# TensorE's expert loop gets one turn ahead of the first expert, and the rank products and the first gather stand inside it

## The chip, the cores and the metric

One core of one Trainium2 chip runs the kernel, one launch. The metric is the device time of that core in microseconds, the median of the runs; smaller is better.

## What is computed

Two transformer blocks over 256 tokens of width 1024, in f32. The change touches the last stage, a mixture of 32 experts, of which every token uses four:

```
logits = t @ w_router + b_router
top_val, top_idx = lax.top_k(logits, TOP_K)          # 4 of 32
gate_w = jax.nn.softmax(top_val, axis=-1)
...
xb = t_pad[tok_idx]                                   # the tokens of one expert
hb = xb @ w_exp_in[e] + b_exp_in[e]                   # 1024 x 2048
g, u = jnp.minimum(hb[:, :F], 7.0), jnp.clip(hb[:, F:], -7.0, 7.0)
a = g * jax.nn.sigmoid(1.702 * g) * (u + 1.0)
return a @ w_exp_out[e] + b_exp_out[e]                # 1024 x 1024
...
y = jnp.einsum('nk,nkd->nd', gate_w, y_slot)
```

## The kernel before

The weights of an expert are 12 MB: 8 MB of `w_exp_in` (in `big_mem`, four pieces of two rows k, semaphores `win_in`) and 4 MB of `w_exp_out` (four pieces, `wout_in`). There is one place for them on the chip. The queue of SyncE (SP) writes a piece of the next expert (L430, L433) as soon as TensorE (PE) has counted up `gu_part` or `y_part` for the piece that it replaces. The first expert's pieces are loaded before the loop (L413, L416).

Before the loop PE sums the logits; VectorE (DVE) makes from them the choice `sel` (L2022, `sel_ready`) and the gates. PE then multiplies `sel` with a triangle and with ones (L908 to L912: the rank of each token in its expert, `rank_ps`), transposes the gates (L917), and DVE makes from the ranks the selection `picks` of the first expert (L2040). With it PE gathers that expert's tokens (L1025, L1026; the matmuls stand in L936). Then PE reads from `further` how many tokens the first expert has, and enters `pe.Fori(0, E)` at L1071.

A turn of the loop is one expert. Its body holds the same pass three times, written out for up to 32, 64 and 96 tokens (`GROUPS[0]`, `[1]`, `[2]`), and conditional branches jump over those that don't apply: L1083 over the first, L1086 over the second, L1088 over the third; L1096 jumps over `bias_out`, and L1071 goes back to the loop's start. A pass is: the first product (`gu`, L953, waits for `win_in`), the gather of the next expert's tokens (L936), transposes (L974, L982), the second product (`second`, L994, waits for `wout_in`) and the sum into the output banks (`combine`, L1008, L1017). The first expert in the loop takes the pass for 64 tokens, the second that for 32. DVE, ScalarE (ACT) and SP have loops of their own, which the change leaves as they are.

PE's program is read in blocks of 16 KB by a DMA queue of its own (q8, kind "instruction").

Of the kernel before, what the change touches and what calls it, by code (L numbers as in the profile page):

```python
# [16 lines left out]
P = 128  # L17
D = 1024
SEQ = 256
T = SEQ // P  # L20
KD = D // P
# [4 lines left out]
E = 32  # L26
# [4 lines left out]
TRIO = 3  # L31
SLOTS = TRIO * XS
PASSES = -(-SEQ // SLOTS)
TURNS = E + -(-SEQ * 4 // SLOTS) + 1
EARLY = 5
GROUPS = (((0, XS),), ((0, 2 * XS),), ((0, 2 * XS), (2 * XS, XS)))
# [85 lines left out]
def program(nc, ins, out):  # L122
# [3 lines left out]
    with ExitStack() as ctx:  # L126
        s = {n: ctx.enter_context(nc.semaphore(n)) for n in EVENTS}
# [114 lines left out]
        sel = sb("sel", T, E)  # L242
        gate = sb("gate", T, E + 1)
# [6 lines left out]
        further = sb("further", 2, E + 1, dt=I32)  # L250
# [3 lines left out]
        order = sb("order", E + 1, dt=I32)  # L254
# [3 lines left out]
        ident = stay[:, IDENT:IDENT + P]  # L258
        aeye = stay[:, AEYE:AEYE + P]
        tri = stay[:, TRI:TRI + P]  # L260
        ones = stay[:, ONES:ONES + P]

        ps = ctx.enter_context(nc.psum_tensor("ps", [P, 8, 512], F32))
# [213 lines left out]
        def _(pe):  # L477
            mm = nc.tensor.matmul
# [130 lines left out]
            for g in range(2):  # L609
                for k in range(KD):  # L610
                    for z in range(2):
                        mm(ps[HEAD * z:HEAD * (z + 1), 2, SEQ * g:SEQ * (g + 1)], cols8[1][:, k, HEAD * g:HEAD * (g + 1)], hT[:, k, :],
                           start=(k == 0), stop=(k == KD - 1))
            for t in range(T):
                for k in range(KD):
                    last = mm(ps[:, 3, P * t:P * (t + 1)], hT[:, k, P * t:P * (t + 1)], cols8[1][:, k, P:2 * P],
                              start=(k == 0), stop=(k == KD - 1))
# [27 lines left out]
            for r in range(2):  # L645
                b = 4 + 2 * r
                pe.wait_ge(s["pv_out"], 3 + r)
                for m in range(2):
                    hd = 2 * r + m
                    mm(ps[:, b + m, 0:SEQ], m1["krT"][:, hd, 0:P], m1["qrT"][:, hd, :], start=True, stop=True)  # L650
                    last = mm(ps[:, b + m, SEQ:KEYS], m1["krT"][:, hd, P:SEQ], m1["qrT"][:, hd, P:SEQ], start=True, stop=True)
                last.then_inc(s["inner_ps"], 1)
            for r in range(2):
                b = 4 + 2 * r
                pe.wait_ge(s["decay_ready"], r + 1)
                for m in range(2):
# [5 lines left out]
                    last = mm(ps[:, b, SEQ + P * m:SEQ + P * (m + 1)], w[:, SEQ:KEYS], v[1], start=False, stop=True)  # L662
# [14 lines left out]
            for hd in range(RET_HEADS):  # L677
                for t in range(T):
                    last = nc.tensor.transpose(ps[:, 5 + 2 * (hd // 2), 256 * (hd % 2) + P * t:256 * (hd % 2) + P * (t + 1)],
                                               m1["ret"][:, t, P * hd:P * (hd + 1)], ident)  # L680
# [19 lines left out]
            with pe.Fori(0, NF // 2) as j:  # L700
                for u in range(2):
                    pe.wait_ge(s[f"conv{u}"], j + 1)
                    for g in range(2):
                        b = 2 * u + g
                        pe.wait_ge(s[f"lo{b}"], j + 1)
                        for k in range(KD):
                            if u == 0 and g == 0 and k % 4 == 0:
                                pe.wait_ge(s["hT_lo"], KD + 2 * k)
                            last = three(ps[:, 4 + u, SEQ * g:SEQ * (g + 1)], quarter(w_hi, b)[:, k, :], quarter(w_lo, b)[:, k, :],
                                         hT_hi[:, k, :], hT_lo[:, k, :], k == 0, k == KD - 1)  # L710
# [22 lines left out]
            for t in range(T):  # L733
                for n in range(2):
                    for k in range(NF - 4, NF):
                        if t == 0 and n == 0:
                            pe.wait_ge(s[f"lo{k % 4}"], NF // 2 + k // 4 + 1)
                        last = down(k, t, [n])
# [8 lines left out]
            for i in range(4):  # L747
                last = mm(ps[:, i, :], stay[:, FLIP:FLIP + P], toep_flipped[:, 2 * i:2 * i + 2, :], start=True, stop=True)
# [76 lines left out]
            for hd in range(4):  # L825
                for t in range(T):
                    last = nc.tensor.transpose(ps[:, hd // 2, 256 * (hd % 2) + P * t:256 * (hd % 2) + P * (t + 1)],
                                               m2["oD"][:, t, P * hd:P * (hd + 1)], ident)
# [3 lines left out]
            for i in range(4):  # L832
                for side, (x_hi, x_lo, x_ready, w_ready) in enumerate(((oa_hi, oa_lo, "oa_lo", "c_lo_a"), (ob_hi, ob_lo, "ob_lo", "c_lo_b"))):
                    p = 2 * i + side
# [38 lines left out]
            for t in range(T):  # L873
                for q in range(4, 8):
                    pe.wait_ge(s["q_lo"], q - 1)
                    last = closing(q, t)
# [27 lines left out]
            for n in range(2):  # L904
                residual(1, n)

            pe.wait_ge(s["sel_ready"], 1)
            mm(ps[:, 5, 0:E], tri, sel[:, 0, :], start=True, stop=True)  # L908
            mm(ps[:, 5, E:2 * E], ones, sel[:, 0, :], start=True, stop=False)
            mm(ps[:, 5, E:2 * E], tri, sel[:, 1, :], start=False, stop=True)  # L910
            mm(ps[:, 5, 2 * E:3 * E], ones, sel[:, 0, :], start=True, stop=False)
            mm(ps[:, 5, 2 * E:3 * E], ones, sel[:, 1, :], start=False, stop=True).then_inc(s["rank_ps"], 1)  # L912


            pe.wait_ge(s["gates_done"], 1)
            for t in range(T):
                last = nc.tensor.transpose(ps[0:E, 4, P * t:P * (t + 1)], gate[:, t, 0:E], ident)  # L917
            last.then_inc(s["gateT_ps"], 1)

            def bias_out():  # L920

                pe.wait_ge(s["gateT_ready"], 1)
# [8 lines left out]
            def gather(lo, hi, bank=7):  # L931

                for k in range(lo, hi):
                    c = SLOTS * (k % EARLY)
                    for t in range(T):
                        last = mm(ps[:, bank, c:c + SLOTS], h1[:, t, SEQ * (k // 2) + k % 2:SEQ * (k // 2 + 1):2], moe["picks"][:, t, :], start=(t == 0), stop=(t == T - 1))  # L936
                if hi in (EARLY, KD):
                    last.then_inc(s["gather_ps"], 1)
# [82 lines left out]
                        pe.wait_ge(s["combined"], 2 * nth + 2)  # L1021

            pe.sem_inc(s["combined"], 1)
            pe.wait_ge(s["picks_ready"], 1)
            gather(0, EARLY)  # L1025
            gather(EARLY, KD, 6)  # L1026
            pe.wait_ge(s["gateT_ready"], 1)
            pe.wait_ge(s["counts_ready"], 1)
            pe.wait_ge(s["bias_zeroed"], 2)
            pe.wait_ge(s["bias_split"], 2)  # L1030
            base_reg, turn_reg = pe.alloc_register("pe_base"), pe.alloc_register("pe_turn")
            pe.reg_mov(base_reg, 0)
            pe.reg_mov(turn_reg, 0)
# [1 line left out]
            def one_pass(blocks, landed_all, load_next):  # L1035

                base = pe.snap(base_reg, min_val=0, max_val=2 * TURNS)
                turn = pe.snap(turn_reg, min_val=0, max_val=2 * TURNS)
                pe.wait_ge(s["xT_ready"], 2 * turn + 1)
                pe.wait_ge(s["own_ready"], turn + 1)  # L1040
                gu(blocks, landed_all, 2 * turn + 2)
                pe.wait_ge(s["picks_ready"], turn + 2)
                gather(0, EARLY)
                load_next()
                for b, (at, m) in enumerate(blocks):
                    pe.wait_ge(s["source_ready"], base + b + 1)
                    pe.wait_ge(s["u_ready"], base + b + 1)
                    way_back(b, at)
                for b, (at, m) in enumerate(blocks):
                    pe.wait_ge(s["back_ready"], base + b + 1)  # L1050
                    pe.wait_ge(s["a_ready"], base + b + 1)
                    turn_a(at, m)
                pe.wait_ge(s["xT_ready"], 2 * turn + 3)
                gather(EARLY, EARLY + 1)
                pe.wait_ge(s["aT_ready"], base + len(blocks))
                second(blocks, landed_all)
                gather(EARLY + 1, EARLY + 2)
                for b, (at, m) in enumerate(blocks):
                    pe.wait_ge(s["y_ready"], base + b + 1)
                    combine(b, at, m, base + b)  # L1060
                gather(EARLY + 2, KD)
                pe.reg_add(base_reg, base_reg, len(blocks))
                pe.reg_add(turn_reg, turn_reg, 1)

            extra_reg, more_reg, next_extra, next_more = (pe.alloc_register("pe_" + z) for z in ("extra", "more", "next_extra", "next_more"))
            pe.reg_mov(extra_reg, pe.value_load(further[0:1, 0, 0:1], min_val=0, max_val=TRIO - 1))
            pe.reg_mov(more_reg, pe.value_load(further[0:1, 1, 0:1], min_val=0, max_val=PASSES - 1))
            nth_reg = pe.alloc_register("pe_nth")
            for r in (next_extra, next_more, nth_reg):
                pe.reg_mov(r, 0)  # L1070
            with pe.Fori(0, E) as e:  # L1071
                landed_all = 16 * e + 16
                extra = pe.snap(extra_reg, min_val=0, max_val=TRIO - 1)
                more = pe.snap(more_reg, min_val=0, max_val=PASSES - 1)

                def load_next():

                    pe.wait_ge(s["order_ready"], 1)
                    following = pe.value_load(order[0:1, bass.ds(e + 1, 1)], min_val=0, max_val=E)
                    pe.reg_mov(next_extra, pe.value_load(further[0:1, 0, bass.ds(following, 1)], min_val=0, max_val=TRIO - 1))  # L1080
                    pe.reg_mov(next_more, pe.value_load(further[0:1, 1, bass.ds(following, 1)], min_val=0, max_val=PASSES - 1))

                with pe.If(extra < 1):  # L1083
                    one_pass(GROUPS[0], landed_all, load_next)
                with pe.If(extra > 0):
                    with pe.If(extra < 2):  # L1086
                        one_pass(GROUPS[1], landed_all, load_next)
                    with pe.If(extra > 1):  # L1088
                        with pe.Fori(0, PASSES) as p:
                            with pe.If(more >= p):  # L1090
                                one_pass(GROUPS[2], landed_all, load_next)
                            pe.nop()
                        pe.nop()
                    pe.nop()
                pe.nop()
                with pe.If_eq(nth_reg, E // 2):  # L1096
                    bias_out()
                pe.reg_add(nth_reg, nth_reg, 1)
                pe.reg_mov(extra_reg, next_extra)
                pe.reg_mov(more_reg, next_more)  # L1100
# [1113 lines left out]
```

## Time and profile before

| | |
|---|---|
| median of 3 runs | 1506.52 us (1506.22 to 1511.2) |
| the profiled execution | 1507.34 us |
| its span | 1505.5 us |
| mean granted TensorE clock | 0.976 |
| PE busy | 1339.8 us (89%) |
| DVE, ACT, POOL busy | 448.4, 359.8, 139.0 us |
| read from HBM | 492.76 MB, 328 GB/s over the span |
| q8, instruction | 26 packets, 0.43 MB |

The span runs from the first to the last instruction of the profiled execution, whose own time is 1.8 us longer. The experts' weights are 384 MB of the 493 MB read. A stall of the engine's instruction stream shows in the profile as idle time "issue" before the engine's next instruction, and as the duration of the branch itself on the sequencer (PEldq).

### The profile page before, as it was taken

The numbers are of one execution on the slowest core, as the hardware profiler recorded it, in microseconds if no ns is written. First come the engines' busy times: TensorE is split into PE (matmuls) and PEld (weight loads), VectorE is DVE, ScalarE is ACT, GpSimd is POOL, SyncE is SP. The second block draws the span as 40 slices with busy tenths as digits, with TensorE's granted clock in tenths as the row PEclk, the third lists the DMA queues.
The fourth block names the chain that finished last, engine by engine and source line by source line (L and its number), as shares of the span: only waits on it lengthen the run. The fifth ranks groups of instructions, "written<-read, shape, count | busy, mean of one in ns | idle before, by whom it ended". The sixth has DMA issues, their size and how long they took to land.

```text
span 1505.5 us, 25303 instructions
## 1 busy us (share of the span) xinstructions
PE 1339.8 (89%) x9344; PEld 801.1 (53%) x9345; DVE 448.4 (30%) x906; ACT 359.8 (24%) x690; POOL 139.0 (9%) x65
## 2 busy tenths in 40 slices
PE   7999999998999898988998888998889988889865
PEld 6454999887989863434343333343334333433432
DVE  1326677745543771111111111111011111111112
ACT  1234666545566520101000100010001001000101
POOL 0000122005765400000000000000000000000000
PEclk9999999999999999999999999999999999999997
DMA  9442466855344478999999999999999999999996
GB/s 342 152 129 56 118 190 181 320 195 187 135 147 168 168 285 364 429 425 427 424 411 426 429 426 426 424 412 425 427 424 428 411 425 426 428 428 424 407 427 258
DMA packets 113493, 494.35 MB, mean 328 GB/s; under 512 B 7617, under 2 KB 55089, under 8 KB 80465
## 3 DMA queue, kind: packets, MB, share of 16 engines
q1 hardware_dynamic: 111971, 491.50, 81.5%
q10 hardware_dynamic: 1486, 2.34, 0.4%
q8 instruction: 26, 0.43, 0.1%
q14 instruction: 10, 0.08, 0.0%
HBM read 492.76 MB, written 1.06 MB: 328 GB/s over the span
## 4 chain that ended last, share of the span: by engine, by line
PE 59%; DMA 33%; DVE 3%; ACT 2%; issue 2%; SPq 0%; DVEq 0%; ACTq 0%
DMA big_mem<-in_w_exp_in 29%; PE ps L953 16%; PE ps L994 6%; PE ps L696 5%; PE ps L698 5%; PE ps L697 5%; PE ps L524 4%; PE ps L936 4%; DMA big_mem<-in_w_exp_out 3%; PE ps L668 2%; PE ps L720 1%; PE ps L722 1%; PE ps L721 1%; PE ps L1017 1%; PE ps L513 1%
## 5 line engine op out<-in xcount | busy, mean ns | idle before, releaser
L953 PE MATMUL ps<-big_mem,ring_mem 128*32 128x512 f32 (+1 forms) x2304 | 382.4, 640 | 67.7 <-DMA big_mem<-in_w_exp_in 67.7
L953 PEld LDWEIGHTS ps<-big_mem,ring_mem 128*32 128x32 f32 (+1 forms) x2304 | 112.6, 125 | 313.2 <-issue 200.8
L994 PE MATMUL ps<-big_mem,x 128*32 128x256 f32 (+1 forms) x1888 | 181.9, 430 | 8.3 <-DMA big_mem<-in_w_exp_out 4.5
L696 PE MATMUL ps<-hT_hi,w_hi 128*128 128x256 f32 x600 | 171.2, 285 | 1.3 <-DVE hT_lo L1619 1.3
L936 PEld LDWEIGHTS ps<-ring_mem,h 128*128 128x128 f32 x1056 | 137.3, 200 | 62.5 <-issue 61.3
L698 PE MATMUL ps<-hT_hi,w_lo 128*128 128x256 f32 x600 | 169.8, 283 | 0.0
L697 PE MATMUL ps<-hT_lo,w_hi 128*128 128x256 f32 x600 | 169.8, 283 | 0.0
L936 PE MATMUL ps<-ring_mem,h 128*128 128x96 f32 x1056 | 154.7, 291 | 0.9 <-DVE ring_mem L2040 0.9
L2081 DVE TENSOR_SCALAR ring_mem<-ps 128x256 f32<-128x256 f32 (+1 forms) x36 | 18.7, 520 | 429.9 <-PE ps L953 429.9
L1524 ACT ACTIVATE ring_mem<-ring_mem 128x256 f32<-128x256 f32 (+1 forms) x36 | 17.7, 493 | 492.0 <-DVE ring_mem L2081 492.0
L994 PEld LDWEIGHTS ps<-big_mem,x 128*32 128x32 f32 (+1 forms) x1888 | 70.6, 115 | 105.8 <-issue 64.7
L696 PEld LDWEIGHTS ps<-hT_hi,w_hi 128*128 128x128 f32 x600 | 115.1, 192 | 4.8 <-issue 3.1
L1528 ACT ACTIVATE ring_mem<-ps 128x480 f32<-128x480 f32 x66 | 32.4, 490 | 349.2 <-PE ps L936 349.2
L697 PEld LDWEIGHTS ps<-hT_lo,w_hi 128*128 128x128 f32 x600 | 115.1, 192 | 0.0
L698 PEld LDWEIGHTS ps<-hT_hi,w_lo 128*128 128x128 f32 x600 | 115.1, 192 | 0.0
L461 POOL TENSOR_TENSOR w_lo<-ring_mem,w_hi 128x1024 fp32r<-128x1024 f32 x38 | 92.1, 2434 | 114.3 <-DVE w_lo L1872 78.7
L2097 DVE COPY ring_mem<-ps 128x256 f32<-128x256 f32 (+1 forms) x36 | 18.4, 520 | 263.8 <-PE ps L994 263.8
L524 PE MATMUL ps<-ring_mem,hT 128*128 128x512 f32 x128 | 56.0, 595 | 0.0
L2071 DVE TENSOR_SCALAR ring_mem<-stay,posb,gate 128x128 f32<-128x128 f32 x72 | 21.3, 343 | 106.7 <-PE ps L936 88.4
L456 POOL TENSOR_TENSOR w_lo<-ring_mem,w_hi 128x1024 fp32r<-128x1024 f32 x11 | 26.8, 2439 | 211.8 <-ACT w_hi L1260 211.8
L1260 ACT ACTIVATE w_hi<-ring_mem 128x1024 fp32r<-128x1024 f32 x44 | 44.9, 1051 | 0.0
L1833 DVE SCALAR_TENSOR_TENSOR big_mem<-ps,cols,big_mem 128x255 f32<-128x255 f32 (+1 forms) x88 | 38.4, 477 | 17.6 <-ACT big_mem L1292 13.4
(335 smaller groups left out, 1465.2 us busy)
## 6 DMA issues: line engine op xcount, KB each, us to landing
big_mem<-in_w_exp_in SPq DMA_DIRECT2D x128, 2048.0 KB, 22.7
big_mem<-in_w_exp_out SPq DMA_DIRECT2D x128, 1024.0 KB, 22.5
ring_mem<-in_w_in SPq DMA_DIRECT2D x15, 2048.0 KB, 8.0
ring_mem<-in_w_up SPq DMA_DIRECT2D x44, 512.0 KB, 5.0
ring_mem<-in_w_down SPq DMA_DIRECT2D x5, 2048.0 KB, 8.7
ring_mem<-in_w_out SPq DMA_DIRECT2D x4, 2048.0 KB, 8.1
ring_mem<-in_w_branch_a SPq DMA_DIRECT2D x1, 2048.0 KB, 7.5
ring_mem<-in_w_branch_b SPq DMA_DIRECT2D x1, 2048.0 KB, 7.6
```

The lines of the kernel that those rows point to most:

```text
L461: nc.gpsimd.tensor_tensor(split_piece(w2_lo, p), piece(p), split_piece(w2_hi, p).bitcast(F32), ALU.subtract).then_inc(s["m2_lo"], 1)
L524: last = mm(ps[:, bank + t, :], hT[:, k, P * t:P * (t + 1)], cols8[n % 3][:, k, :], start=(k == 0), stop=(k == KD - 1))
L668: last = mm(ps[:, 2 * t + n, :], m1["catT"][:, k, P * t:P * (t + 1)], cols8[(6 + n) % 3][:, k, :], start=(k == 0), stop=(k == KD - 1))
L696: mm(out, hi, x_hi, start=start, stop=False)
L697: mm(out, hi, x_lo, start=False, stop=False)
L698: return mm(out, lo, x_hi, start=False, stop=stop)
L936: last = mm(ps[:, bank, c:c + SLOTS], h1[:, t, SEQ * (k // 2) + k % 2:SEQ * (k // 2 + 1):2], moe["picks"][:, t, :], start=(t == 0), stop=( ...
L953: last = mm(out, stationary, weights[:, f, w * q:w * (q + 1)] if m > XS else weights[:, :, w * q:w * (q + 1)], start=start, stop=stop)
L994: last = mm(ps[m * q:m * (q + 1), 4 + at // XS, 0:w], aT[:, k % n, k // n, :], wout[:, k, w * q:w * (q + 1)], start=(k == 0), stop=(k == K ...
L1260: run(quarter(w_hi, b), up_slot[u][:, :, g, :], ACT.Copy).then_inc(s[f"hi{b}"], 1)
L1528: run(moe["xT"][:, lo:hi, :].rearrange("p k m -> p (k m)"), ps[:, bank, 0:(hi - lo) * SLOTS], ACT.Copy).then_inc(s["xT_ready"], 1)
L1833: last = v.scalar_tensor_tensor(c, ps[:, 4 + u, SEQ * g:SEQ * (g + 1) - i], cols[:, bass.ds(tap + f, 1)], c, ALU.mult, ALU.add)
```

## The change

The block from the rank products to the reading of `further` becomes a function `opening`. The loop has E + 1 turns. In the first turn `extra` is 3 (TRIO), a value that no expert has, and the branches lead past all three passes to `opening`; it leaves the first expert's counts in `next_extra` and `next_more`. The counters are moved by one: `landed_all` is 16 * e, `order` is read at e, and `bias_out` comes at turn E // 2 + 1. The third pass stands under one test more (`extra < TRIO`), and a test behind it (`extra > TRIO - 1`) guards `opening`.

```diff
-            pe.wait_ge(s["sel_ready"], 1)
-            mm(ps[:, 5, 0:E], tri, sel[:, 0, :], start=True, stop=True)
...
-            last.then_inc(s["gateT_ps"], 1)
...
             pe.sem_inc(s["combined"], 1)
-            pe.wait_ge(s["picks_ready"], 1)
-            gather(0, EARLY)
-            gather(EARLY, KD, 6)
-            pe.wait_ge(s["gateT_ready"], 1)
-            pe.wait_ge(s["counts_ready"], 1)
-            pe.wait_ge(s["bias_zeroed"], 2)
-            pe.wait_ge(s["bias_split"], 2)
...
-            pe.reg_mov(extra_reg, pe.value_load(further[0:1, 0, 0:1], min_val=0, max_val=TRIO - 1))
-            pe.reg_mov(more_reg, pe.value_load(further[0:1, 1, 0:1], min_val=0, max_val=PASSES - 1))
+
+            def opening():
+
+                pe.wait_ge(s["sel_ready"], 1)
+                mm(ps[:, 5, 0:E], tri, sel[:, 0, :], start=True, stop=True)
...
+                last.then_inc(s["gateT_ps"], 1)
+
+                pe.wait_ge(s["picks_ready"], 1)
+                gather(0, EARLY)
+                gather(EARLY, KD, 6)
...
+                pe.reg_mov(next_extra, pe.value_load(further[0:1, 0, 0:1], min_val=0, max_val=TRIO - 1))
+                pe.reg_mov(next_more, pe.value_load(further[0:1, 1, 0:1], min_val=0, max_val=PASSES - 1))
+
+            pe.reg_mov(extra_reg, TRIO)
+            pe.reg_mov(more_reg, 0)
...
-            with pe.Fori(0, E) as e:
-                landed_all = 16 * e + 16
-                extra = pe.snap(extra_reg, min_val=0, max_val=TRIO - 1)
+            with pe.Fori(0, E + 1) as e:
+                landed_all = 16 * e
+                extra = pe.snap(extra_reg, min_val=0, max_val=TRIO)
...
                     with pe.If(extra > 1):
-                        with pe.Fori(0, PASSES) as p:
-                            with pe.If(more >= p):
-                                one_pass(GROUPS[2], landed_all, load_next)
+                        with pe.If(extra < TRIO):
+                            with pe.Fori(0, PASSES) as p:
+                                with pe.If(more >= p):
+                                    one_pass(GROUPS[2], landed_all, load_next)
+                                pe.nop()
                             pe.nop()
+                        with pe.If(extra > TRIO - 1):
+                            opening()
                         pe.nop()
                     pe.nop()
                 pe.nop()
-                with pe.If_eq(nth_reg, E // 2):
+                with pe.If_eq(nth_reg, E // 2 + 1):
                     bias_out()
```

On PE, ahead of the loop, the program of before has these rows (L908 to L912 the rank products, L917 the gates' transposes, L936 the gather, L1066 and L1067 the counts; L1071 is the loop's start and L1083 its first branch):

```order
-L908 MATMUL ps<-sel,stay 128x32
-L909 MATMUL ps<-sel,stay 128x32
-L910 MATMUL ps<-sel,stay 128x32
-L911 MATMUL ps<-sel,stay 128x32
-L912 MATMUL ps<-sel,stay 128x32
-L917 MATMUL ps<-stay,gate 32x128 x2
-L936 MATMUL ps<-ring_mem,h 128x96 x16
-L1066 TENSOR_LOAD further
-L1066 ISA x2
-L1067 TENSOR_LOAD further
-L1067 ISA x2
-L1071 UNCONDITIONAL_BRANCH
```

At the same place the changed program goes from the last rows ahead of the loop (L890 is `residual`) straight to the loop's start and its first branch (now L1089), behind which the first pass stands (L940 is the old L953):

```order
L890 MATMUL ps<-h,stay 128x512
L902 MATMUL ps<-stay,ring_mem 128x32 x2
L890 MATMUL ps<-h,stay 128x512 x2
L1077 UNCONDITIONAL_BRANCH
L1077 ISA
L1089 COMPARE_AND_BRANCH
L1017 ISA
L1020 REGISTER_ALU
L940 MATMUL ps<-ring_mem 32x512 x4
```

The moved rows stand behind the third pass, at the end of the loop's body (L1095 closes the third pass, L1101 guards `opening`, L923 is the gather):

```order
+L1095 UNCONDITIONAL_BRANCH
+L1101 COMPARE_AND_BRANCH
+L1050 MATMUL ps<-sel,stay 128x32
+L1051 MATMUL ps<-sel,stay 128x32
+L1052 MATMUL ps<-sel,stay 128x32
+L1053 MATMUL ps<-sel,stay 128x32
+L1054 MATMUL ps<-sel,stay 128x32
+L1059 MATMUL ps<-stay,gate 32x128 x2
+L923 MATMUL ps<-ring_mem,h 128x96 x16
+L1069 TENSOR_LOAD further
+L1069 ISA x2
+L1070 TENSOR_LOAD further
```

So the same instructions are issued in the same order, but three passes' code lies between the loop's start and them. Counted over the program's listing (a f32 matmul row is two weight loads and two matmuls), the first pass is some 400 instructions of PE, the second some 330, the third some 650; the whole program has some 6,550.

## Rows read from the trace of the kernel before

**Rows 1.** The page: busy time of PE, DMA queues, the chain's shares.

```profile
PE 1339.8 (89%) x9344; PEld 801.1 (53%) x9345; DVE 448.4 (30%) x906; ACT 359.8 (24%) x690; POOL 139.0 (9%) x65
...
q8 instruction: 26, 0.43, 0.1%
```

**Rows 2.** Windows: length, busy of PE, PEld, DVE, ACT, POOL; clock, DMA share, GB/s.

```profile
549.75:561.00 11.25, 11.14 (x60) 7.83 (x61) 8.10 (x20) 2.26 (x3) 0.00 (x0) 0.85 0.13 34
561.00:591.00 30.00, 23.75 (x128) 11.46 (x129) 5.38 (x14) 2.59 (x5) 0.00 (x0) 0.96 0.98 410
591.00:596.00 5.00, 5.00 (x32) 1.23 (x28) 0.00 (x0) 0.00 (x0) 0.00 (x0) 0.55 0.25 61
596.00:1461.50 865.50, 751.77 (x5632) 336.39 (x5624) 117.63 (x324) 72.49 (x161) 0.00 (x0) 0.97 1.00 423
```

**Rows 3.** Timeline of PE from 545 to 600: start, us, instruction, idle before.

```profile
545.61 0.59 PE L890 MATMUL ps<-h,stay 128*128 128x512 f32 x1
547.36 0.41 PE L908 MATMUL ps<-sel,stay 128*128 128x32 f32 x2 [1.16 <-DVEq L2024]
...
549.75 5.54 PE L936 MATMUL ps<-ring_mem,h 128*128 128x96 f32 x32 [0.88 <-DVE ring_mem L2040]
555.40 0.64 PE L953 MATMUL ps<-ring_mem 128*64 128x512 bf16 x4
...
590.56 0.62 PE L953 MATMUL ps<-ring_mem 128*32 128x512 bf16 x4 [5.01 <-issue]
```

**Rows 4.** The branch L1088 on PE's sequencer: duration min/median/max in ns, first and last start.

```profile
L1088 PEldq COMPARE_BRANCH  x13: 73/210/6063, 583.1 to 1345.1; - x13
```

**Rows 5.** The same of L1083, L1096, L1029.

```profile
L1083 PEldq COMPARE_BRANCH  x32: 68/80/367, 554.5 to 1463.8; - x32
L1096 PEldq COMPARE_BRANCH  x32: 70/207/252, 589.2 to 1493.3; - x32
L1029 PEldq EVENT_SEMAPHORE  x1: 51/51/51, 551.8 to 551.8; - x1
```

**Rows 6.** Timeline of SP's queue: the issues of expert weights, 559 to 596.

```profile
559.55 10.63 SPq L430 DMA_DIRECT2D big_mem<-in_w_exp_in  x4
576.94 5.48 SPq L433 DMA_DIRECT2D big_mem<-in_w_exp_out  x4
594.80 0.35 SPq L430 DMA_DIRECT2D big_mem<-in_w_exp_in  x1
```

**Rows 7.** DMA queues from 551.5 to 553.5: packets, MB, share.

```profile
q8 instruction: 1, 0.02, 2.7%
```

**Rows 8.** DMA queues from 555.5 to 557.

```profile
q8 instruction: 1, 0.02, 3.6%
```

**Rows 9.** DMA from 583 to 586.5: all packets, none of q8.

```profile
DMA packets 213, 1.49 MB, mean 426 GB/s; under 512 B 31, under 2 KB 31, under 8 KB 31
```

**Rows 10.** DMA queues from 586.5 to 588.

```profile
q8 instruction: 1, 0.02, 4.5%
```

**Rows 11.** DMA queues from 591 to 592.5.

```profile
q8 instruction: 1, 0.02, 4.4%
```

**Rows 12.** DMA queues from 770 to 1500, all that moved.

```profile
q1 hardware_dynamic: 28116, 304.09, 99.0%
```

**Rows 13.** Windows of 5 us after each third pass (columns as in rows 2).

```profile
772.00:777.00 5.00, 5.00 (x48) 1.34 (x44) 0.00 (x0) 0.00 (x0) 0.00 (x0) 0.90 0.88 310
980.50:985.50 5.00, 5.00 (x48) 1.36 (x44) 0.00 (x0) 0.00 (x0) 0.00 (x0) 0.93 0.88 298
1189.00:1194.00 5.00, 5.00 (x48) 1.45 (x44) 0.00 (x0) 0.00 (x0) 0.00 (x0) 0.96 0.88 315
1397.00:1402.00 5.00, 5.00 (x51) 1.37 (x45) 0.00 (x0) 0.00 (x0) 0.00 (x0) 0.94 0.82 275
```

**Rows 14.** PE's waits, the whole run: us in total, times, longest.

```profile
PE ps L953 <- DMA big_mem<-in_w_exp_in: 67.7, 46, 3.0
```

More of the change, by code:

```diff
@@ L905, in _ @@
                 residual(1, n)
-            pe.wait_ge(s["sel_ready"], 1)
-            mm(ps[:, 5, 0:E], tri, sel[:, 0, :], start=True, stop=True)
[L909 to L917, printed above, removed]
-            last.then_inc(s["gateT_ps"], 1)
             def bias_out():
@@ L1065, in _ @@
             extra_reg, more_reg, next_extra, next_more = (pe.alloc_register("pe_" + z) for z in ("extra", "more", "next_extra", "next_more"))
-            pe.reg_mov(extra_reg, pe.value_load(further[0:1, 0, 0:1], min_val=0, max_val=TRIO - 1))
-            pe.reg_mov(more_reg, pe.value_load(further[0:1, 1, 0:1], min_val=0, max_val=PASSES - 1))
+            def opening():
+                pe.wait_ge(s["sel_ready"], 1)
+                mm(ps[:, 5, 0:E], tri, sel[:, 0, :], start=True, stop=True)
+                mm(ps[:, 5, E:2 * E], ones, sel[:, 0, :], start=True, stop=False)
+                mm(ps[:, 5, E:2 * E], tri, sel[:, 1, :], start=False, stop=True)
+                mm(ps[:, 5, 2 * E:3 * E], ones, sel[:, 0, :], start=True, stop=False)
+                mm(ps[:, 5, 2 * E:3 * E], ones, sel[:, 1, :], start=False, stop=True).then_inc(s["rank_ps"], 1)
+                pe.wait_ge(s["gates_done"], 1)
+                for t in range(T):
+                    last = nc.tensor.transpose(ps[0:E, 4, P * t:P * (t + 1)], gate[:, t, 0:E], ident)
+                last.then_inc(s["gateT_ps"], 1)
+                pe.wait_ge(s["picks_ready"], 1)
+                gather(0, EARLY)
+                gather(EARLY, KD, 6)
+                pe.wait_ge(s["gateT_ready"], 1)
+                pe.wait_ge(s["counts_ready"], 1)
+                pe.wait_ge(s["bias_zeroed"], 2)
+                pe.wait_ge(s["bias_split"], 2)
+                pe.reg_mov(next_extra, pe.value_load(further[0:1, 0, 0:1], min_val=0, max_val=TRIO - 1))
+                pe.reg_mov(next_more, pe.value_load(further[0:1, 1, 0:1], min_val=0, max_val=PASSES - 1))
+            pe.reg_mov(extra_reg, TRIO)
+            pe.reg_mov(more_reg, 0)
             nth_reg = pe.alloc_register("pe_nth")
@@ L1078, in load_next @@
                     pe.wait_ge(s["order_ready"], 1)
-                    following = pe.value_load(order[0:1, bass.ds(e + 1, 1)], min_val=0, max_val=E)
+                    following = pe.value_load(order[0:1, bass.ds(e, 1)], min_val=0, max_val=E)
                     pe.reg_mov(next_extra, pe.value_load(further[0:1, 0, bass.ds(following, 1)], min_val=0, max_val=TRIO - 1))
```

## The prediction

> **What bounds the kernel now.** I read the page first: PE is busy 89% of the span, and its code comes in 26 packets of 16 KB over q8 [rows 1]; 6,550 instructions in 26 packets are some 250 in each. Then the windows [rows 2]. From 596 to 1461.5 the DMA engines are full, at 423 GB/s: the weights of the remaining experts set the time, and PE waits for them 67.7 us in all [rows 14]. So the end moves with the time lost by the weights' stream, not with PE. The stream stands still twice. From 549.75 to 561 it waits for PE's first use of the first expert's weights (34 GB/s). From 591 to 596 it waits for the second expert (61 GB/s). Against 423 GB/s the second gap costs 5 x (1 - 61/423) = 4.3 us. Third, at four places behind the long third pass a window of 5 us moves 275 to 315 GB/s [rows 13]: there the stream waits for PE too.
>
> Why the second gap is there: PE ends the first expert at 585.6 and starts the next at 590.56, idle 5.01 us, "issue" [rows 3]. In that time the branch L1088 takes 6.06 us, where its median is 0.21 [rows 4]. It starts at 583.1 and jumps over the third pass, 650 instructions or 2.6 blocks, to code that has not yet been read. No packet of q8 starts up to 586.5, one does between 586.5 and 588 [rows 9, 10], and the branch ends at 583.1 + 6.06 = 589.15. Then SP may replace the first piece only at 594.80 [rows 6], 4.2 us after PE's start at 590.56, partly at the clock's lower level: the window 591 to 596 has a granted clock of 0.55, between 1.2 and 2.4 GHz [rows 2].
>
> **What the change does to this.** The arithmetic and its order stay. What is new is the way to `opening`: from the loop's start PE's sequencer jumps over the first pass (400 instructions, 1.6 blocks), over the second (330, 1.3 blocks) and over the third (650, 2.6 blocks). The third is the jump that took 6.06 us. So the cold read of the loop's end is not removed; it goes ahead of the first expert, and two more jumps over unread code go with it. The question is how much of that is hidden.
>
> *The cover.* PE's last matmul before the loop starts at 545.61, and L908 at 547.36, having waited 1.16 us for `sel` [rows 3]. The sequencer may be through with the rows before some tenths earlier; I take 545 for the first jump. So 2.4 us are hidden behind the choice of experts.
>
> *First jump.* The weights of w_exp_out still land until 549.75, so the price is that of the jump beside a busy stream: 6.06 us [rows 4], to 551.1. Is its target unread? In the trace before, the same jump (L1083) took 0.367 us, against 0.21 for a usual taken branch [rows 5], at 554.5, with a block read between 551.5 and 553.5 [rows 7]. The extra 0.16 us say that the block was ready only at about 554.7: it was the very block of the target, ordered when the sequencer crossed into the block before it. In the changed program the loop's start lies 100 instructions earlier (the moved rows) and, by my count, short of that border. So nothing has ordered it. Bounds: 0 (read ahead after all) to 6.06; I take 6.06.
>
> *Second jump.* The packet that follows a missed one: after the packet of 586.5 to 588 came the next from 591 to 592.5 [rows 10, 11], beside a busy stream. With the stream idle a packet ordered at 554.5 lies in 555.5 to 557 [rows 8], so about 1.2 us pass from order to start, and the block of rows 7 was ready some 2.5 us after its start at the earliest 551.5 (I take 2.5, since 589.15 less 586.6 is the same). If it is ordered as the first ends, at 550, it is ready at 550 + 1.2 + 2.5 = 553.7. Price 2.6; bounds 0 and 6.06.
>
> *Third jump.* Cold for certain: target 2.6 blocks ahead, as in rows 4, but the stream is idle by then: 1.2 + 2.5 = 3.7 us, or 4.7 if a read-ahead of the block between goes first. I take 4.2: `opening` starts at 553.7 + 4.2 = 557.9. Bounds 3.7 and 6.06. L908 starts 557.9 - 547.36 = 10.5 us late.
>
> *From `opening` to the first expert.* Before, L908 to the first L953 took 555.40 - 547.36 = 8.0 us, and the gather's matmuls and the sequencer's own work (from L1029 at 551.8) ended together [rows 3, 5]. Now the sequencer also closes a turn: two taken branches of 0.21 [rows 5] and some register work. The same way at 589.15 to 590.56 took 1.4 us, of which half replaces what stood before: +0.7. After 10 us of idleness the clock is at 1.2 GHz as it was after 5 us (rows 2: 0.55 from 591 to 596), for the gather and perhaps the first matmuls: +0.8. The first expert's start is 12.0 us late, and with it the whole DVE chain, `order_ready` and SP's first order (559.55 before).
>
> *Given back.* At the first expert's end the loop's end is read and the blocks of the first pass have been passed: no stall of 5.01 us, and the second gap of 4.3 us goes. PE reaches the second expert 0.9 us behind the first, and its first piece is free 2.3 us on, at the upper clock, while 12 MB at 423 GB/s take 28 us: the stream has no gap there.
>
> *Per turn.* The third pass gets one test more ahead (0.07) and one taken branch behind (0.21). Where that pass is taken, four times, the stream already waits [rows 13]: 4 x 0.28 = 1.1 us. In other turns branches hide behind 0.7 us of queued gather.
>
> **Sum.** 12.0 - 4.3 + 1.1 = +8.8 us. The profiled execution, 1507.34 (span 1505.5), becomes 1516.1; it lies 0.8 above the median of the runs, so the median goes from 1506.52 to 1515.3.
>
> **A rule weighed.** Rows 4 show one dear jump and rows 5 many cheap ones, backwards too. The Trainium skill, "Runtime: NRT & Kernel Launch", section "Instruction fetch mechanics", says that a taken branch whose target isn't in the current window of two blocks forces a read before execution goes on. For the first turn it says what I take, all three jumps beyond a border; for later turns it would make each way round the loop a stall, before and after. The trace disagrees there: from 770 to 1500 q8 moved nothing [rows 12]. The same section of the Trainium skill puts PE's store at 128 KiB, eight such blocks.
>
> **Rivals.**
> 1. *The way is cheap.* Blocks are read further ahead than I think, or the sequencer starts on the way so early that the choice of experts hides it. Then only the second gap goes: -4.3 + 0.7 + 1.1 = -2.5, 1504.0. For it: the jump of 0.367 us. Against it: rows 4, the third jump is the same one. This ends as not slower; it decides if the three jumps together cost less than 2.4 + 2.5 = 4.9 us.
> 2. *One dear jump.* First and second are read ahead, the third costs 6.06 beside the busy stream: 545.4 + 6.06 = 551.5, 4.1 late, with +0.7, +0.8: 5.6 - 4.3 + 1.1 = +2.4, 1508.9. With two dear jumps, +5 to +6, 1512. For it: the way was paid once before. Against: the three targets lie in three blocks.
> 3. *All three at the full price.* 545 + 18.2 = 563.2, 15.8 late: 17.3 - 4.3 + 1.1 = +14.1, 1520.6. Against: the stream is idle from 549.75.
> 4. *The loop no longer fits.* Its body was some 1,410 instructions, and spans some 1,515 now: from six blocks to seven, eight with the one read ahead. If the store holds fewer, every way round costs a read of about 5 us, 32 x 5 = 160 us, less at most the 67.7 us that PE now waits [rows 14]: +90, some 1600. For it: nothing but the size; against: rows 12, with a body nearly as long. By the eight blocks of the Trainium skill (same page and section) it would just fit.
>
> **Chances.** Forecast (dear first jump, two cheaper behind, +6.5 to +12) 0.50; one or two dear jumps (+1 to +6.5) 0.25; cheap way 0.10; full price or a loss of more than +12 without the gain 0.11; no fit 0.04. A measurement tells about 0.5%, 7.5 us, from no change. The forecast lies near that edge, a quarter of it below: slower 0.38 + 0.11 + 0.04 = 0.53, and 0.02 of the two-jump case, 0.55. Faster needs -7.5, more than the second gap gives: 0.03. Same 0.42. Range: 1504 (cheap way) to 1521 (full price), which leaves out 0.1.
>
> **What would show it.** After: PE idle "issue" or a wait ahead of the rank products (now L1050) of some 10 us after the last L890, where 1.16 us stood; three long branches near 545 to 558 (L1089, L1092, L1095), with durations of about 6, 2.5 and 4; the first SP order of the loop near 571.5, not 559.55; no idle of 5.01 ahead of the second expert; a full stream from there on. Wrong if L1050 starts before 552 (rival 2 or 1), if the gap of 591 to 596 is still there behind the first expert (its price moved and paid twice), or if q8 has packets in later turns (rival 4).

## The result and the profile after

The changed kernel takes 1516.39 us in the median of 6 runs (1515.68 to 1520.66), the kernel before 1506.37 in its 6 (1502.88 to 1511.2): ratio 1.0069, with an interval of 1.0049 to 1.0089. That is 10.0 us slower, a little over the 0.5% that can be told from no change. The profiled execution took 1516.32 us, its span is 1514.5, 9.0 more than before.

First the branches of the first turn on PE's sequencer, in the changed kernel (duration in ns min/median/max, first and last start):

```profile
L1089 PEldq COMPARE_BRANCH  x33: 71/80/6096, 543.6 to 1472.8; - x33
L1091 PEldq COMPARE_BRANCH  x33: 73/210/228, 549.8 to 1502.0; - x33
L1092 PEldq COMPARE_BRANCH  x14: 67/68/3293, 549.9 to 1353.7; - x14
L1094 PEldq COMPARE_BRANCH  x14: 73/213/225, 553.3 to 1354.0; - x14
L1095 PEldq COMPARE_BRANCH  x5: 73/73/4730, 553.4 to 1354.1; - x5
```

Each of the three jumps over a pass has one long execution, its first: 6.10, 3.29 and 4.73 us, 14.1 in all, one behind the other from 543.6 to 558.1. L1094, which has L1088's place of before, is never over 0.225 us; the 6.06 of [rows 4] is gone from there. What PE makes of it (timeline of PE):

```profile
558.31 0.63 PE L1050 MATMUL ps<-sel,stay 128*128 128x32 f32 x2 [13.38 <-issue]
...
561.25 0.42 PE L1053 MATMUL ps<-sel,stay 128*128 128x32 f32 x1 [1.25 <-issue]
561.49 0.62 PE L1054 MATMUL ps<-sel,stay 128*128 128x32 f32 x2
...
563.20 5.64 PE L923 MATMUL ps<-ring_mem,h 128*128 128x96 f32 x32 [0.67 <-DVE ring_mem L2050]
570.02 0.65 PE L940 MATMUL ps<-ring_mem 128*64 128x512 bf16 x4 [1.19 <-ACT ring_mem L1538]
...
599.42 0.71 PE L923 MATMUL ps<-ring_mem,h 128*128 128x96 f32 x4
600.06 0.41 PE L940 MATMUL ps<-ring_mem 128*32 128x512 bf16 x4
```

The rank products start after 13.38 us of idleness, where 1.16 stood in [rows 3], and stand still once more for 1.25 us in the middle of L1053: a block of code begins to be read at the opening's start (between 558 and 564 q8 has two packets, the first near 558.8). The first expert starts at 570.02 (555.40 before), the second right behind it at 600.06, with no idle time: the 5.01 us of [rows 3] are gone. The weights' stream in windows (busy of PE, PEld, DVE, ACT, POOL; clock, DMA share, GB/s):

```profile
548.50:575.60 27.10, 14.19 (x72) 10.29 (x73) 9.34 (x25) 2.64 (x4) 0.00 (x0) 0.69 0.09 23
575.60:605.00 29.40, 28.20 (x168) 12.60 (x169) 5.12 (x14) 2.59 (x5) 0.00 (x0) 1.00 0.98 412
605.00:1470.00 865.00, 746.48 (x5612) 332.68 (x5604) 117.17 (x323) 72.73 (x161) 0.00 (x0) 0.98 1.00 423
```

Against [rows 2] there is one gap instead of two: 27.1 us at 23 GB/s instead of 11.25 at 34 and 5 at 61. Behind it the stream is full at the same 423 GB/s. SP's orders, first of the changed kernel:

```profile
574.18 10.63 SPq L430 DMA_DIRECT2D big_mem<-in_w_exp_in  x4
591.52 5.48 SPq L433 DMA_DIRECT2D big_mem<-in_w_exp_out  x4
602.40 5.47 SPq L430 DMA_DIRECT2D big_mem<-in_w_exp_in  x4
...
738.84 16.79 SPq L430 DMA_DIRECT2D big_mem<-in_w_exp_in  x4
...
782.76 5.48 SPq L430 DMA_DIRECT2D big_mem<-in_w_exp_in  x4
...
1446.53 0.34 SPq L430 DMA_DIRECT2D big_mem<-in_w_exp_in  x1
```

and the orders for the same experts in the kernel before:

```profile
729.47 16.79 SPq L430 DMA_DIRECT2D big_mem<-in_w_exp_in  x4
...
773.49 5.48 SPq L430 DMA_DIRECT2D big_mem<-in_w_exp_in  x4
...
1437.42 11.56 SPq L430 DMA_DIRECT2D big_mem<-in_w_exp_in  x3
```

The first order is 14.6 us later than in [rows 6]. That of 602.40 is only 7.6 later than the 594.80 before, but the stream before had run dry by then and this one had not, so orders are compared where both streams are full. From 738.84 against 729.47 (9.4) over 782.76 against 773.49 (9.3) to 1446.53 against 1437.42 (9.1) the distance stays: all of the loss is made ahead of the first expert, and 5.4 us of it are given back in the first turns.

### The profile page after: what moved, and what is told of

Same layout as the page of the kernel before. It is cut to its first block, busy times and chain, and to the rows that moved or that the text cites. A ratio compares the mean times of both kernels' runs of the same rounds, so it can differ in the third digit from the quotient of the medians.

```text
span 1514.5 us, 25323 instructions
## 1 busy us (share of the span) xinstructions
PE 1335.2 (88%) x9344; PEld 797.6 (53%) x9345; DVE 448.4 (30%) x906; ACT 360.2 (24%) x690; POOL 139.2 (9%) x65
## 4 chain that ended last, share of the span: by engine, by line
PE 58%; DMA 34%; issue 3%; DVE 3%; ACT 2%; SPq 0%; DVEq 0%; ACTq 0%
DMA big_mem<-in_w_exp_in 27%; PE ps L940 14%; PE ps L981 6%; DMA big_mem<-in_w_exp_out 6%; PE ps L696 5%; PE ps L698 5%; PE ps L697 5%; PE ps L524 4%; PE ps L923 3%; PE ps L668 2%; PE ps L720 1%; PE ps L722 1%; PE ps L721 1%; PE ps L1004 1%; PE ps L513 1%
## 5 line engine op out<-in xcount | busy, mean ns | idle before, releaser
L940 PE MATMUL ps<-big_mem,ring_mem 128*32 128x512 f32 (+1 forms) x2304 | 376.2, 628 | 70.3 <-DMA big_mem<-in_w_exp_in 70.3
L940 PEld LDWEIGHTS ps<-big_mem,ring_mem 128*32 128x32 f32 (+1 forms) x2304 | 110.9, 123 | 313.8 <-issue 197.8
L923 PEld LDWEIGHTS ps<-ring_mem,h 128*128 128x128 f32 x1056 | 136.2, 198 | 60.8 <-issue 59.7
L923 PE MATMUL ps<-ring_mem,h 128*128 128x96 f32 x1056 | 153.7, 290 | 0.7 <-DVE ring_mem L2050 0.7
L1843 DVE SCALAR_TENSOR_TENSOR big_mem<-ps,cols,big_mem 128x255 f32<-128x255 f32 (+1 forms) x88 | 38.4, 478 | 17.6 <-ACT big_mem L1302 13.4
```

The costliest lines, as they stand in the source:

```text
L940: last = mm(out, stationary, weights[:, f, w * q:w * (q + 1)] if m > XS else weights[:, :, w * q:w * (q + 1)], start=start, stop=stop)
L1843: last = v.scalar_tensor_tensor(c, ps[:, 4 + u, SEQ * g:SEQ * (g + 1) - i], cols[:, bass.ds(tap + f, 1)], c, ALU.mult, ALU.add)
```

## The experiments

The theory: the way of PE's sequencer over code that it has not read costs one block read per jump, in series, about 6 us beside the weights' stream and 3 to 5 without it; and the stream's second gap before is the one such jump of [rows 4]. "Before" in the measured ratios is the kernel before on the same chip: 1508.5 us in the first four, 1506.2 in the last three; where an expectation names a time, its distance from 1506.4 is what the ratio has to be held against. Single executions of the kernel before lie between 1502.46 and 1513.58 us, so whole times are judged by the ratios, and mechanisms by durations inside a trace.

**One jump to the opening** (`e1_one_jump`)

```diff
+                with pe.If(extra < TRIO):
                     with pe.If(extra < 1):
                         one_pass(GROUPS[0], landed_all, load_next)
...
+                with pe.If(extra > TRIO - 1):
+                    opening()
```

> The changed kernel, but one test (extra < TRIO) stands around all three passes, so that the first turn jumps once over all of them (some 1,400 instructions) to the opening, where it jumped three times. Theory, each jump to an unread block has its own price, one behind the other on the sequencer (6.1, 3.3 and 4.7 us in the changed kernel): only the first stays, 6.1, so the rank products start near 550.1 instead of 558.3. The first pass's code has then not been passed, so the jump over it to the first expert's pass is itself unread now, 3.5 us with an idle stream. Net 4.5 us less than the changed kernel: 1512. Rival A, the price goes by the distance jumped: the one jump costs about 14 us, 1516 or above. Rival B, the extra turn and its code in the loop cost the time, not the jumps: 1516.

Measured: 1527.96 us, ratio 1.0123 (1.0091 to 1.0154), slower than every forecast. The branches:

```profile
L1089 PEldq COMPARE_BRANCH  x33: 77/80/6084, 544.9 to 1485.5; - x33
L1090 PEldq COMPARE_BRANCH  x32: 65/65/3642, 562.5 to 1485.6; - x32
L1095 PEldq COMPARE_BRANCH  x13: 73/210/6747, 597.1 to 1366.5; - x13
L1103 PEldq COMPARE_BRANCH  x33: 73/208/5594, 551.1 to 1514.4; - x33
```

The two prices that the theory named are there: one jump over 1,400 instructions costs 6.08, no more than one over 400 (rival A falls), and the jump over the first pass then costs 3.64. But the jump over the third pass at the first expert's end costs 6.75 us again, though the code behind it was read 50 us earlier for the opening. PE's timeline shows two more stalls, 9.32 us ahead of the second expert and 10.72 ahead of the fourth, and q8 has ten packets from 600 on (three in the kernel before):

```profile
608.91 0.62 PE L940 MATMUL ps<-ring_mem 128*32 128x512 bf16 x4 [9.32 <-issue]
671.41 0.62 PE L940 MATMUL ps<-ring_mem 128*32 128x512 bf16 x4 [10.72 <-issue]
```

The branches in narrower windows tell what they are made of (L1103 guards the opening: behind the third pass it jumps over it):

```profile
L1103 PEldq COMPARE_BRANCH  x1: 3278/3278/3278, 603.9 to 603.9; - x1
L1095 PEldq COMPARE_BRANCH  x1: 6042/6042/6042, 658.2 to 658.2; - x1
L1103 PEldq COMPARE_BRANCH  x2: 212/2903/5594, 664.3 to 690.3; - x2
```

6.75 and 3.28 stand in a row ahead of the second expert, 6.04 and 5.59 ahead of the fourth: the jump over the third pass is paid at the end of two experts. So a block once read need not be there later. That was not in the theory, and it is why neither its 1512 nor a rival's 1516 came out; `e6_opening_first` goes after it.

**The empty turn, the opening outside** (`e2_empty_turn`)

```diff
+            opening()
             with pe.Fori(0, E + 1) as e:
...
-                        with pe.If(extra > TRIO - 1):
-                            opening()
```

> The changed kernel, but the opening stands ahead of the loop again and the loop's first turn is empty: it only takes the three jumps, behind the issued gather. Theory: the jumps start near 553.6, with the stream idle, and cost about 3.7, 3.3 and 4.7, so that the first expert starts near 566.6 (555.4 before); less the second gap of 5.4 us it is 1513. Rival B, that the opening's place inside the loop (its own code, the clock after the long idle time) costs the time and not the way there: only the second gap goes, 1502.

Measured: 1512.03 us, ratio 1.0025 (1.0010 to 1.0041), and 4.0 us over the kernel before by the spans (1509.5). By the ratio that is 3.8 us over, where the expectation was 6.5. Rival B, 4 to 5 us under the kernel before, falls: the way alone, without the moved code, makes it slower.

```profile
L1089 PEldq COMPARE_BRANCH  x33: 68/80/468, 553.6 to 1467.9; - x33
L1092 PEldq COMPARE_BRANCH  x14: 67/68/3222, 554.3 to 1348.8; - x14
L1094 PEldq COMPARE_BRANCH  x14: 73/210/222, 557.6 to 1349.1; - x14
L1095 PEldq COMPARE_BRANCH  x5: 73/73/4494, 557.8 to 1349.2; - x5
```

The first jump costs 0.47 us, not 3.7: with the opening ahead of it the loop's start lies where it lay before, and its target is read in time as in [rows 5, 7]. The first expert starts at 563.96 after 8.59 us of idleness, earlier than the 566.6 expected, by that jump.

**No weights beside the first jump** (`e3_wout_late`)

```diff
             sp.wait_ge(s["out_ps"], T)
+            sp.wait_ge(s["counts_ready"], 1)
             for k in range(KD // 2):
                 sp.dma_start(wout[:, 2 * k:2 * k + 2, :], wout_x[0, k]).then_inc(wout_in[k], 16)
 
-            sp.wait_ge(s["counts_ready"], 1)
```

> The changed kernel, but SP asks for the first expert's w_exp_out only behind counts_ready, so that no weights move while PE takes the first jump. Theory, an unread block costs 6.1 us beside a busy stream and about 3.7 beside an idle one: L1089's longest branch falls to 3.7, the other two stay at 3.3 and 4.7, the start of the first expert and the end come 2.4 us earlier, 1514.0. Rival: the price of a jump doesn't depend on the weights' stream and the three differ for another reason: L1089 stays at 6.1 and the time at 1516.4.

Measured: 1514.22 us, ratio 1.0041 (1.0025 to 1.0057), span 1511.3. This kernel's window beside the first jump (columns as above):

```profile
542.00:549.50 7.50, 2.98 (x10) 1.20 (x8) 4.67 (x25) 2.03 (x4) 0.00 (x0) 1.00 0.02 4
```

its branches:

```profile
L1089 PEldq COMPARE_BRANCH  x33: 71/80/3318, 543.6 to 1469.7; - x33
L1092 PEldq COMPARE_BRANCH  x14: 67/68/3153, 547.1 to 1350.7; - x14
L1095 PEldq COMPARE_BRANCH  x5: 72/73/4777, 550.5 to 1351.1; - x5
```

and the changed kernel's window:

```profile
542.00:548.50 6.50, 2.93 (x10) 1.20 (x8) 4.62 (x25) 1.97 (x4) 0.00 (x0) 1.00 1.01 420
```

With 4 GB/s beside it instead of 420 the first jump takes 3.32 us instead of 6.10, the other two stay. The price of an unread block depends on the weights' stream by 2.8 us. SP's first order of the loop comes at 571.45 instead of 574.18, 2.7 us earlier (2.4 expected), and the span is 3.2 us shorter; the two ratios, 1.0041 and 1.0069, have intervals that just overlap.

The traces also show where the 2.8 us lie. In the changed kernel no packet of q8 starts from 543.6 to 547.3, and one does from 547.3 to 547.5; with the late weights none starts from 543.6 to 544.6, and one does from 544.6 to 544.8 (packets, MB and share in these two short windows):

```profile
q8 instruction: 1, 0.02, 31.2%
q8 instruction: 1, 0.02, 29.9%
```

Beside the full stream the block's packet starts 3.7 us after the branch, without it 1.0; from the packet's start to the branch's end it is 2.4 and 2.3 us. The stream delays the start of the read, not the read.

**The second pass's end behind the third pass** (`e4_tail_behind`, again as `e4b_tail_again`)

```diff
                     with pe.If(extra < 2):
-                        one_pass(GROUPS[1], landed_all, load_next)
+                        head(GROUPS[1], landed_all, load_next)
                     with pe.If(extra > 1):
...
+                    with pe.If(extra < 2):
+                        tail(GROUPS[1])
```

> The kernel before, but the end of the second pass (the last gathers and the sum into the output) is written behind the third pass's code, so that the cold jump over the third pass comes while PE still has the 32 matmuls of the second product queued. Theory, the second gap in the weights' stream is due to the 6.06 us branch and to nothing else: the branch takes as long, but behind 7 us of queued work, PE's idle 5.01 us ahead of the second expert goes, the gap at 591 goes with it, and the time falls by 5.4 us to 1501.0. Rival C, the stall only moves (the queue holds less work than that, or the last gather waits instead): between 1504 and 1506.4.

> The kernel with the second pass's end behind the third pass's code, once more, beside the next one: 5.0 us under the kernel before, as its first run had it, with PE idle 1.8 us ahead of the last gather of the first expert.

Measured: 1503.78 us, ratio 0.9967 (0.9948 to 0.9986), and 1501.04, ratio 0.9970 (0.9952 to 0.9989): 4.5 to 5 us under the kernel before, where 5.4 and 5.0 were expected. The branch (first run):

```profile
L1097 PEldq COMPARE_BRANCH  x13: 73/210/5950, 577.6 to 1341.1; - x13
```

and PE's timeline:

```profile
574.96 7.09 PE L994 MATMUL ps<-big_mem,x 128*64 128x512 f32 x32 [0.24 <-ACT x L1548]
583.85 0.68 PE L936 MATMUL ps<-ring_mem,h 128*128 128x96 f32 x4 [1.80 <-issue]
...
588.32 0.62 PE L953 MATMUL ps<-ring_mem 128*32 128x512 bf16 x4
```

The cold branch is as long as before, but hides behind matmuls already issued, all but 1.80 us (I had counted on 7 us of queued work; from 577.6 to the end of L994 at 582.05 there were 4.5). The idle time ahead of the second expert is gone: the second gap came from this one branch. Rival C is right in part: 1.80 us of the stall moved to the last gather (2.10 in the second run), and the stream still dips, to 321 GB/s from 590 to 596.

**The same, split earlier** (`e5_split_early`): the head ends after `gu`'s third row k.

```diff
-                gu(blocks, landed_all, 2 * turn + 2)
+                gu(blocks, landed_all, 2 * turn + 2, 0, 3)
...
+                gu(blocks, landed_all, 2 * turn + 2, 3, KD)
```

> The kernel before, but of the second pass only the start (the waits and the first product up to its third row k) stays where it was, and the rest stands behind the third pass's code. The cold jump then comes near 558, before SP's first order of the loop at 559.55, beside an idle stream. Theory: it costs 3.3 to 3.7 us instead of 6, behind 4 to 5 us of queued matmuls, so that PE is idle 0.5 us or less where it was idle 1.8 with the later split; 1.3 us under that one, 6.3 under the kernel before. Rival: a jump's price is 6 here too, the first product of the first expert then stands still for 1.5 to 2 us, and it equals the later split.

Measured: 1503.10 us, ratio 0.9982 (0.9966 to 0.9998). The branch L1099:

```profile
L1099 PEldq COMPARE_BRANCH  x13: 73/210/3799, 556.6 to 1338.9; - x13
```

and SP's orders:

```profile
559.42 10.63 SPq L430 DMA_DIRECT2D big_mem<-in_w_exp_in  x4
...
587.69 5.47 SPq L430 DMA_DIRECT2D big_mem<-in_w_exp_in  x4
```

The branch takes 3.80 us beside an idle stream and no idle time is left; the third expert's weights are ordered at 587.69, 7.1 us ahead of [rows 6] and 3.2 ahead of the later split (590.91), and the stream has no dip (431 GB/s from 590 to 596). By the spans the two splits are equal (1499.4 and 1499.1 to 1499.2), by the medians the later one is 2 us better, with overlapping intervals: the 1.3 us that I expected of the earlier one were not found, and of 6.3 under the kernel before the ratio shows 2.7. The lead is lost on the way: SP's last group of orders for `w_exp_in` begins at 1431.37, at 1431.38 with the later split. Where and why is open. Both beat both kernels: the intervals of their ratios end below 1.

**The opening first, one jump behind it** (`e6_opening_first`)

```diff
+                with pe.If(extra > TRIO - 1):
+                    opening()
                 with pe.If(extra < TRIO):
                     with pe.If(extra < 1):
```

> The changed kernel, with the opening at the start of the loop's body (reached without a jump) and one test around all three passes, so that the first turn jumps once over them, behind the issued gather, and then over the first pass. Both jumps are unread and beside an idle stream: the first expert starts 7 to 8 us late. Theory M, a block that lies behind the last one read makes the blocks after it be read again: the first pass's blocks are read after the loop's end, so the jump over the third pass costs 6 us once more, the second gap stays, and there are more packets of q8 later, as with the one jump to the opening; 8 to 12 us over the kernel before. Rival K, that kernel's second gap came from its store being too small for the longer way or from the place of the opening at the end: here the second gap goes, no more than 3 us over the kernel before.

Measured: 1513.52 us, ratio 1.0048 (1.0033 to 1.0063), 7.2 us over the kernel before, a little less than the 8 to 12 expected. The branches (L1091 over all passes, L1092 over the first, L1097 over the third):

```profile
L1091 PEldq COMPARE_BRANCH  x33: 72/73/3782, 552.2 to 1470.6; - x33
L1092 PEldq COMPARE_BRANCH  x32: 65/68/427, 557.4 to 1470.7; - x32
L1097 PEldq COMPARE_BRANCH  x13: 72/210/6265, 588.6 to 1351.3; - x13
```

and PE's timeline:

```profile
596.53 0.62 PE L940 MATMUL ps<-ring_mem 128*32 128x512 bf16 x4 [5.48 <-issue]
```

The jump to the loop's end was paid (3.78), and at the first expert's end it is paid again (6.27); the second gap stays. Here the code's length and the place of the opening are others than in the one-jump kernel, and nothing but the skipped middle is shared. The empty turn, which reached the loop's end step by step, has 0.222 at the same branch (L1094). So rival K falls.

Two things are not as expected. The jump over the first pass was cheap (0.43), so SP's first order was only 5.5 us late (565.06) and the first expert itself 3.0 (558.39). And there are not more packets of q8 from 600 on, as theory M had it after the ten of the one-jump kernel, but the three of the kernel before:

```profile
q8 instruction: 3, 0.05, 0.0%
```

## Why the prediction was right

The time lies 1.1 us from the forecast (1516.39 against 1515.3), and the mechanism is the forecast's, but the sum owes part of its closeness to errors that cancel. The closeness is also finer than the measurement: the ratio's interval is 7.4 to 13.4 us over the kernel before.

- **What bounds the kernel, and the gap's cause.** Right. Of the two kernels that hide the branch of [rows 4] one loses the second gap whole (`e5_split_early`), the other keeps a dip (`e4_tail_behind`), and both are faster.
- **The cover and the first jump.** Right: 543.6 to 549.7, 6.10 us against 6.06, begun 1.4 us earlier than forecast. The stretch ahead of the loop ended 1.3 us earlier in this execution (L890's last matmuls start at 542.97, at 544.24 before), as it also did with the empty turn and the late weights but not with the one jump; no edit accounts for it, and the sum counts it apart.
- **Second and third jump.** Right in kind, both under-sized: 3.29 against 2.6, and 4.73 against 4.2. The 2.6 rests on a slip: the first jump was put to end at 551.1, but the next block was taken as ordered at 550; from 551.1 the same 1.2 + 2.5 give 3.7. For the third, 4.7 was the alternative in which a block between is read first, and two packets of q8 do start inside that branch (from 553.4 to 558.1). The dependence on the stream, which split 6 from 3.7, is shown by the late weights.
- **From the opening to the first expert.** Mis-sized: 11.7 us against 9.5 (8.0 before). Not foreseen was a fourth wait for code, 1.25 us inside the rank products, with the packet of q8 near 558.8; it is there with the late weights (1.20) and the one jump (1.81) too, and not with the opening outside. With a granted clock of 0.55 from 548.5 to 561, near the 1.2 GHz level, the rank products took some 1.3 us more, and the turn's closing 1.1 instead of 0.7.
- **The first expert's delay.** 14.6 us by the clock of the trace, 15.9 with the 1.3 of the stretch ahead; forecast 12.0.
- **Given back.** 5.4 us against 4.3: I had priced only the window from 591 to 596, and the stream's restart behind it is slow too (335 GB/s from 595.5 to 600). The 5.4 is the first order's 14.6 less the later 9.2; the windows give it by themselves as 4.3 for 591 to 596 and 0.95 for 596 to 598 (221 GB/s), 5.2. The forecast's 28 us for an expert's weights take 12 MB as 12 million bytes; they are 12.6 million, 29.7 us, and the conclusion holds all the more.
- **Per turn.** Wrong: +1.1 forecast, nothing found (the orders are 9.4 us late in the first run of the third pass, 9.1 behind the last).
- **Sum.** 15.9 - 1.3 - 5.4 + 0 = 9.2, and the spans differ by 9.0 (since the 5.4 comes from the same distances, the independent check is the 5.2 of the windows, which gives 9.4); forecast 12.0 - 4.3 + 1.1 = 8.8. The delay was taken 3.9 us too small, and three others (1.1 of the gap, 1.1 of the turns, 1.3 of the stretch ahead) went the other way.
- **The rivals.** A cheap way, one dear jump and all at full price are excluded by the three durations. The loop fits: q8 has no packet from 600 on in the changed kernel, three before, all in the first run of the third pass.
- **The rule weighed.** The Trainium skill, "Runtime: NRT & Kernel Launch", section "Instruction fetch mechanics", says that a taken branch to a block outside the current window of two has to wait until that block is read. The first jumps over unread code agree (3.15 to 6.25 us in these runs; 0.37 to 0.47 where the target had been ordered already). Later turns don't: from 600 us on no branch of PE takes more than 0.23 us in the kernel before or in the changed one.

## What to carry to other kernels

A branch over code that has not run yet costs 3 to 7 us of TensorE's sequencer here, once for each place in another block, whatever the distance, and again where code earlier in the loop is read after it (`e1_one_jump`, `e6_opening_first`); a turn ahead that only walks the way collects these prices in a row instead of removing them. Put such a jump where 4 to 5 us of issued matmuls hide it, or where no transfer runs. When a stream of weights is the bound, count what it loses: a stall ahead of its first order lengthens a gap that is there already, and costs in full all the same.

## What the runs showed of the hardware that was not expected

- A block that has been read can be unread again. With one jump to the loop's end, and then blocks of its start read behind it, the end cost 6.75 and 6.04 us (`e1_one_jump`) and 6.27 (`e6_opening_first`) once more; reached step by step it cost 0.22. That reading a block that lies earlier in the program than the last one read makes the later ones be read again fits both. It was argued from these runs, not shown by itself. The three late packets of the kernel before fit it too: they come near 725, 746 and 767, one about every 20 us of the third pass's first run, though the jump over it had skipped 2.6 blocks and the end behind it had been read at 587. The empty turn has the same three (near 732, 751 and 774), the changed kernel none; why that one has none is open.
- The same unread block costs 3.3 us without the weights' stream and 6.1 beside it (3.32 and 6.10 for the same branch), and nearly all of the difference is the time until its packet starts (1.0 against 3.7 us).
- TensorE's queue held some 4.5 us of f32 matmuls (64 columns stationary, 512 moving) ahead of a blocked sequencer, not the 7 us of the whole second product (577.6 to 582.05 in `e4_tail_behind`).
